# Seven products for eight of the sixteen k tiles instead of four, in nine tile pairs of a SwiGLU feed-forward

## The chip, the cores and the metric

The kernel runs on one core of a Trainium2 chip, as one launch. The metric is the device time of that core in microseconds. The core has a matrix engine (TensorE, PE in the rows), two engines that do elementwise work (VectorE, or DVE, and ScalarE, or ACT), a third one for it, GpSimd (POOL), and SyncE (SP), which here issues nearly all transfers. The engines run at the same time and wait for each other through semaphores.

## The reference

One layer of a decoder trunk for 256 tokens of width 2048, in float32: a sparse latent attention, and after it a SwiGLU feed-forward with 5632 hidden columns, each followed by a residual sum and a LayerNorm. The change touches only the feed-forward:

```python
def _swiglu(x, w_gate, w_up, w_down):
    return (jax.nn.silu(x @ w_gate) * (x @ w_up)) @ w_down
# of the layer:
x = _layer_norm(DEEPNORM_ALPHA * x + m, ln1_g, ln1_b)
x = _layer_norm(DEEPNORM_ALPHA * x + _swiglu(x, w_gate, w_up, w_down), ln2_g, ln2_b)
```

## The kernel before

**Three matmuls for each product.** TensorE takes its operands in the format F32R, so every float32 operand is kept as two parts: a high part, rounded by a ScalarE copy, and a low part, the rest, which VectorE gets by subtracting the high part from the float32 value. A product is high by high, high by low and low by high. The stationary operand is a 128 x 128 tile of the activations (act_t, s_t), the moving one 512 columns of the weights (w_hi, w_lo).

**Halves and the ring.** Weights arrive by DMA in raw. They are split in pieces of 1024 columns for each partition, called halves here: one ScalarE instruction writes w_hi, one VectorE instruction writes w_lo. Both have room for RING = 4 halves. Half v is split into the place of half v - 4, so ScalarE waits until TensorE has used that one; VectorE waits for ScalarE (hi_done), TensorE for VectorE (lo_done). SyncE's loads wait for lo_done as well, since raw is free when the low part is made.

**Tiles and pairs.** Gate and up are computed in 22 tiles of 256 hidden columns (512 columns of weights with gate and up side by side), over 16 k tiles of 128. Tiles 0 and 1 are computed on their own. The other 20 form ten pairs (p = 1 to 10). A pair has two tiles and two groups of 128 tokens, so it is a 2 x 2 block problem for every two k tiles. Of the 16 k tiles, the first four of each pair are done in the form of Strassen and Winograd: seven block products instead of eight. The sums of activations that this needs (s_t: s1 to s4) are made once, by GpSimd, ahead of pair 1. The sums of weight blocks (t_sum, four of them for each pair) are made by VectorE, in place in raw, between the low parts. Each of the seven product halves is used by 6 matmuls, and each of the 12 plain halves (the other 12 k tiles, for both tiles) by 12. Three ScalarE copies between PSUM banks (seed), one to p5_s, and two VectorE additions of p5_s bring the seven products to the four results.

**What else these engines do in a pair.** Twice for each pair: ScalarE applies silu (silu_step), VectorE multiplies gate by up (gate_up), TensorE transposes the result by four small matmuls (turn_hid), ScalarE and VectorE split the transposed tile into hid_t (hid_hi, hid_lo). All of it is written into the engines' instruction streams by hand, between the halves, and every engine works in order.

**Memory.** xn holds the normalized activations x1 for the residual sum at the end, s_t has its own place, and raw has five slots of 1 MB in this phase: three for plain weights, two for the blocks of the products. Earlier phases use the first four. So one of the two block slots of pair 1 is free only when tile 1 has been split.

## Time and profile before

| | |
|---|---|
| median of 3 runs | 963.92 us (963.87 to 964.64) |
| the profiled execution | 964.98 us, of which its span (first to last instruction) 962.8 us |
| TensorE | busy 949.2 us, 4536 matmuls |
| VectorE | busy 624.6 us |
| ScalarE | busy 486.4 us |
| GpSimd | busy 52.2 us |
| transfers | 183.84 MB, mean 191 GB/s |

An instruction's duration is longer than its share of the time where an engine works on two at once: a matmul of 512 columns is listed with 389 ns in the middle of a pair, but the next one starts sooner than that. So what a group of instructions costs is read from starts, or from the chain that ended last, where instructions in a row are merged. The engine tables give what an engine did; whether that matters depends on whom it keeps waiting.

### The profile page before, as it was taken

To read this page: it belongs to the slowest core of one execution; us is meant where nothing else is said; L and a number is where in the kernel's file an instruction comes from. 1 tells how busy PE (TensorE), PEld (TensorE's weight loads), DVE (VectorE), ACT (ScalarE), POOL (GpSimd) and SP (SyncE) were. 2 spreads that over 40 slices of the span, in tenths; PEclk is the share of its full clock that TensorE was granted. 3 is DMA by queue.
4 is the path that set the end of the run, shared out by engine and by line. 5 is a ranking of instruction groups with operands and counts; after the bars stand their busy time and mean duration, and the time that the engine had idled before them with its cause. 6 is when DMAs were issued, how large, how long until landed. Compare 5 with 4: busy or idle time off the path is not lost.

```text
span 962.8 us, 11466 instructions
## 1 busy us (share of the span) xinstructions
PE 949.2 (99%) x4536; PEld 794.4 (83%) x4536; DVE 624.6 (65%) x750; ACT 486.4 (51%) x644; POOL 52.2 (5%) x49
## 2 busy tenths in 40 slices
PE   9999999999969999999999999999999999999997
PEld 8999988888848888888888888888888888888885
DVE  6687666587556868586776858576745454444556
ACT  5677764452435646464655646364544343343450
POOL 0115520000400000000000000000000000000000
PEclk9999999999969999999999999999999999999999
DMA  9734315592326364654636364553457455464532
GB/s 364 315 136 175 122 55 214 180 392 88 132 87 262 124 270 166 228 197 152 235 115 268 136 253 185 208 216 133 164 206 288 172 220 180 170 225 168 219 131 88
DMA packets 28147, 183.84 MB, mean 191 GB/s; under 512 B 3136, under 2 KB 3648, under 8 KB 8640
## 3 DMA queue, kind: packets, MB, share of 16 engines
q1 hardware_dynamic: 28064, 183.12, 50.5%
q8 instruction: 36, 0.59, 0.2%
q14 instruction: 15, 0.12, 0.0%
q0 software_dynamic: 32, 0.00, 0.0%
HBM read 181.01 MB, written 2.10 MB: 190 GB/s over the span
## 4 chain that ended last, share of the span: by engine, by line
PE 70%; DVE 1%; DMA 0%; ACT 0%; issue 0%; DVEq 0%; ACTq 0%
PE acc L1782 26%; PE acc L1561 25%; PE tp L1782 8%; PE acc L1769 6%; PE tp L1769 4%; PE tp L1738 1%; DMA raw<-in_w_pairs 0%; DVE raw L1254 0%; PE acc L1867 0%; DVE w_lo L1090 0%; DVE w_lo L1242 0%; ACT w_hi L836 0%; ACT w_hi L755 0%; DVE stats L1326 0%; ACT acc L851 0%
## 5 line engine op out<-in xcount | busy, mean ns | idle before, releaser
L1090 DVE TENSOR_TENSOR w_lo<-raw,w_hi 128x1024 fp32r<-128x1024 f32 (+1 forms) x123 | 146.1, 1195 | 133.8 <-ACT w_hi L755 133.1
L1782 PE MATMUL acc<-w_hi,act_t 128*128 128x512 f32 x720 | 227.1, 392 | 0.0
L1561 PE MATMUL acc<-w_hi,hid_t 128*128 128x512 f32 x672 | 207.9, 389 | 0.0
L1249 DVE TENSOR_TENSOR w_lo<-raw,w_hi 128x1024 fp32r<-128x1024 f32 x120 | 145.2, 1224 | 95.8 <-ACT w_hi L845 94.7
L755 ACT ACTIVATE w_hi<-raw 128x1024 fp32r<-128x1024 f32 x116 | 115.9, 1001 | 164.7 <-PE acc L1561 152.3
L845 ACT ACTIVATE w_hi<-raw 128x1024 fp32r<-128x1024 f32 x120 | 126.1, 1060 | 126.3 <-PE acc L1782 111.2
L1782 PEld LDWEIGHTS acc<-w_hi,act_t 128*128 128x128 f32 x720 | 135.2, 188 | 27.8
L1561 PEld LDWEIGHTS acc<-w_hi,hid_t 128*128 128x128 f32 x672 | 126.1, 188 | 26.1
L1782 PE MATMUL acc<-w_lo,act_t 128*128 128x512 f32 x360 | 140.2, 389 | 0.0
L1561 PE MATMUL acc<-w_lo,hid_t 128*128 128x512 f32 x336 | 130.7, 389 | 0.0
L836 ACT ACTIVATE w_hi<-raw 128x1024 fp32r<-128x1024 f32 x70 | 72.9, 1057 | 74.4 <-DVE raw L1254 48.5
L1242 DVE TENSOR_TENSOR w_lo<-raw,w_hi 128x1024 fp32r<-128x1024 f32 x70 | 83.9, 1222 | 35.1 <-ACT w_hi L836 34.0
L1782 PEld LDWEIGHTS acc<-w_lo,act_t 128*128 128x128 f32 x360 | 67.7, 188 | 13.6
L1782 PE MATMUL tp<-w_hi,act_t 128*128 128x512 f32 x240 | 74.7, 389 | 0.0
L1561 PEld LDWEIGHTS acc<-w_lo,hid_t 128*128 128x128 f32 x336 | 63.1, 188 | 13.1
L1561 PE MATMUL acc<-w_hi,o_t 128*128 128x512 f32 x224 | 73.4, 398 | 0.0
L1782 PEld LDWEIGHTS tp<-w_hi,act_t 128*128 128x128 f32 x240 | 45.1, 188 | 9.3
L1561 PEld LDWEIGHTS acc<-w_hi,o_t 128*128 128x128 f32 x224 | 42.1, 188 | 8.6
L1254 DVE TENSOR_TENSOR raw<-raw 128x1024 f32<-128x1024 f32 x40 | 47.9, 1219 | 0.0
L1782 PE MATMUL tp<-w_lo,act_t 128*128 128x512 f32 x120 | 46.7, 389 | 0.0
L1561 PE MATMUL acc<-w_lo,o_t 128*128 128x512 f32 x112 | 43.6, 390 | 0.0
L1769 PE MATMUL acc<-w_hi,act_t 128*128 128x512 f32 x100 | 36.9, 410 | 6.6 <-DVE w_lo L1242 6.6
(226 smaller groups left out, 1273.3 us busy)
## 6 DMA issues: line engine op xcount, KB each, us to landing
raw<-in_w_pairs SPq DMA_DIRECT2D x80, 1024.0 KB, 4.7
raw<-in_w_down SPq DMA_DIRECT2D x32, 1024.0 KB, 4.6
raw<-in_w_out SPq DMA_DIRECT2D x16, 1024.0 KB, 4.8
raw<-in_w_down SPq DMA_DIRECT2D x16, 768.0 KB, 4.0
raw<-in_w_gu SPq DMA_DIRECT2D x8, 1024.0 KB, 7.0
raw<-in_x_w SPq DMA_DIRECT2D x14, 552.0 KB, 6.9
raw<-in_w_uq SPq DMA_DIRECT2D x4, 1024.0 KB, 6.3
raw<-in_w_ukv SPq DMA_DIRECT2D x4, 1024.0 KB, 5.7
```

The costliest lines, as they stand in the source:

```text
L755: act.activation(w_hi[:, (2 * slot + half + shift) % RING, 0:n], raw[:, slot, first:first + n], ACT.Copy).then_inc(hi_done, 1)
L836: act.activation(by_quad(w_hi[:, v_pair(p, n) % RING, :]), quad(block), ACT.Copy).then_inc(hi_done, 1)
L845: act.activation(w_hi[:, v_pair(p, n) % RING, :], raw[:, slot, h % 2 * HALF:(h % 2 + 1) * HALF], ACT.Copy).then_inc(hi_done, 1)
L1090: dve.tensor_tensor(w_lo[:, h, 0:n], raw[:, slot, first:first + n], w_hi[:, h, 0:n], ALU.subtract).then_inc(lo_done, 1)
L1242: dve.tensor_tensor(by_quad(w_lo[:, v % RING, :]), quad(block), by_quad(w_hi[:, v % RING, :]), ALU.subtract).then_inc(lo_done, 1)
L1249: dve.tensor_tensor(w_lo[:, v % RING, :], raw[:, h // 2 % PAIR_RING, h % 2 * HALF:(h % 2 + 1) * HALF], w_hi[:, v % RING, :], ALU.subtract) ...
L1254: dve.tensor_tensor(quad(dst), quad(x), quad(y), ALU.add).then_inc(t_done, 1)
L1561: last = pe.matmul(acc[:, bank0 + t, :], lhs[:, k, x, t * P:(t + 1) * P], part[:, w, n * GC:(n + 1) * GC], start=(start and x == 0 and par ...
L1738: last = pe.transpose(turned[:, c, t * P:(t + 1) * P], hid[:, t, c * P:(c + 1) * P], ident[:])
L1769: last = pe.matmul(out, factor(q, what, x), part[:, v % RING, q * GC:(q + 1) * GC], start=(start and (q, x) == (0, 0) and part is w_hi), s ...
L1782: last = pe.matmul(out[:, t, :], act_t[:, k0 + m, x, t * P:(t + 1) * P], part[:, v % RING, m * GC:(m + 1) * GC], start=False, stop=((h % P ...
```

## The change

In pairs 2 to 10 the seven products cover eight k tiles instead of four (GROUPS_OF is 1 for pair 1 and 2 for the others). A pair then has 14 product halves (product n for block group 0, then for group 1) and 8 plain halves. The block weights get four slots of raw that are theirs alone, the plain weights four places of 512 KB. For the room this takes, s_t lies where xn is; x1 is written to the output tensor in DRAM after it is made, and read back into xn after the products of pair 10. GpSimd makes the activation sums in two rounds, the second during the plain halves of pair 1. Silu, gate_up, and the transposes with their splits stand at other halves. The diff, cut:

```diff
-QUADS = 2
-PAIR_K = 2 * QUADS
+QUADS = 4
 B11, B21, B12, B22 = range(4)
+T1, T3, T2, T4 = range(4)
 S1, S2, S3, S4 = range(4)
+GROUPS_OF = (None, 1) + (2,) * (PAIRS - 2)
 PRODUCTS = 7
-PLAIN = (KD - PAIR_K) // 2
-PAIR_HALVES = PRODUCTS + 2 * PLAIN
-PAIR_RING = 3
-PLAIN_LOADS = PLAIN
-PAIR_SIGNALS = PAIR_HALVES - 2
+PLAIN_SLOTS = 4
+
+
+def products(p):
+    return PRODUCTS * GROUPS_OF[p]
+
+
+def plain_halves(p):
+    return KD - 4 * GROUPS_OF[p]
+
+
+def halves(p):
+    return products(p) + plain_halves(p)
+
+
 V_FFN = 2 * R_FFN
 V_PAIRS = V_FFN + 2 * TILE_HALVES
-V_DOWN = V_PAIRS + PAIR_HALVES * (PAIRS - 1)
+V_PAIR = (None,) + tuple(V_PAIRS + sum(halves(q) for q in range(1, p)) for p in range(1, PAIRS + 1))
...
         xn = sb("xn", [P, TOK, D])
+        s_t = nc.alloc_sbuf_tensor_at("s_t", [P, 2, 4, QUADS, P], F32R, offset=base_x)
...
-            def load_quads(p):
-
-                if p > 1:
-                    sp.wait_ge(lo_done, v_pair(p - 1, PRODUCTS))
-                for q in range(QUADS):
-                    if p == 1 and q == 0:
...
+            def load_quad(p, n):
+                q = quad_slots(p)[n]
+                if p == 1:
+                    pass
+                elif p == 2 and q < 2:
+                    sp.wait_ge(lo_done, V_FFN + TILE_HALVES + 2 * (PLAIN_SLOTS // 2 + q) + 2)
+                else:
+                    sp.wait_ge(lo_done, v_pair(p - 1, products(p - 1)))
+                sp.dma_start(raw[:, PLAIN_SLOTS // 2 + q, :], w_pairs[p - 1][:, n * RAW_ELEMS:(n + 1) * RAW_ELEMS])\
+                  .then_inc(quad_full[q], 16)
...
+                m = PLAIN_BEFORE[p] + n
+                if m < PLAIN_SLOTS:
+                    sp.wait_ge(lo_done, V_FFN + TILE_HALVES + m + 1)
                 else:
-                    sp.wait_ge(lo_done, V_FFN + TILE_HALVES + 2 * n + 2)
-                e0 = (QUADS + n) * RAW_ELEMS
-                sp.dma_start(raw[:, n % PAIR_RING, :], w_pairs[p - 1][:, e0:e0 + RAW_ELEMS])\
-                  .then_inc(raw_full[n % PAIR_RING], 16)
-
-            for p in range(1, PAIRS):
-                if p == 1:
-                    load_plain(p, 0)
-                    load_plain(p, 1)
-                    load_plain(p, 2)
-                    load_quads(p)
-                else:
-                    for n in range(PAIR_RING):
-                        load_plain(p, n)
-                if p < PAIRS - 1:
-                    load_quads(p + 1)
-                for n in range(PAIR_RING, PLAIN_LOADS):
-                    load_plain(p, n)
+                    sp.wait_ge(lo_done, plain_v(m - PLAIN_SLOTS) + 1)
+                e0 = 2 * GROUPS_OF[p] * RAW_ELEMS + n * HALF
+                sp.dma_start(plain_raw(m), w_pairs[p - 1][:, e0:e0 + HALF]).then_inc(plain_full[m % PLAIN_SLOTS], 16)
...
+            load_quad(1, 0)
+            load_quad(1, 1)
+            for n in range(PLAIN_SLOTS):
+                load_plain(1, n)
+            sp.wait_ge(x1_done, TOK * CHUNKS)
+            sp.dma_start(a["out"].rearrange("(t p) d -> p t d", p=P), xn[:]).then_inc(x1_stored, 16)
+            for p in range(1, PAIRS):
+                if p > 1:
+                    for n in range(PLAIN_SLOTS):
+                        load_plain(p, n)
+                for n in range(PLAIN_SLOTS, plain_halves(p)):
+                    load_plain(p, n)
+                    if p < PAIRS - 1:
+                        if n - PLAIN_SLOTS < 2 * GROUPS_OF[p + 1]:
+                            load_quad(p + 1, n - PLAIN_SLOTS)
+                    elif n - PLAIN_SLOTS < 2:
+                        load_down(0, n - PLAIN_SLOTS)
+
+            for b in range(2, RING):
                 load_down(0, b)
+            sp.wait_ge(x1_stored, 16)
+            sp.wait_ge(*used_half(v_pair(PAIRS - 1, products(PAIRS - 1))))
+            sp.dma_start(xn[:], a["out"].rearrange("(t p) d -> p t d", p=P)).then_inc(x1_back, 16)
...
+                seeds = {G + 3: (0, first[:, 0, :], 1.0), 3 * G + 3: (2, second[:, 0, :], -1.0),
+                         5 * G + 3: (4, first[:, 1, :], 1.0)}
+                for j in range(halves(p)):
...
                         if p > 1:
                             hid_hi(2 * p - 2)
                         silu_step(2 * p - 1)
-                    if h == 9:
+                    if j == 5 * G + 4:
                         hid_hi(2 * p - 1)
+                    if j == n_products + plain_halves(p) // 2 + 3:
                         silu_step(2 * p)
+                    if p == 1 and j == n_products + 6:
...
+            def hid_chores(p, j):
+
+                if j == 5:
+                    if p > 1:
+                        hid_lo(2 * p - 2)
+                    gate_up(2 * p - 1)
+                if j == 5 * GROUPS_OF[p] + 4:
+                    hid_lo(2 * p - 1)
+                if j == products(p) + plain_halves(p) // 2 + 3:
+                    gate_up(2 * p)
...
-                lo_product(p, 0, B11)
-                t_sum(B11, B11, B12)
-                t_sum(B12, B12, B22)
-                lo_product(p, 1, B11)
-                t_sum(B11, B11, B22)
-                lo_product(p, 2, B11)
-                lo_product(p, 3, B21)
-                t_sum(B21, B11, B21)
-                lo_product(p, 4, B12)
-                lo_product(p, 5, B22)
-                lo_product(p, 6, B21)
...
+                groups = range(GROUPS_OF[p])
+                for n in range(PRODUCTS):
+                    for g in groups:
+                        lo_product(p, n, g)
+                        if n == 0:
+                            t_sum(p, g, B11, B11, B12)
+                        if n == 3:
+                            t_sum(p, g, B21, B11, B21)
+                        hid_chores(p, GROUPS_OF[p] * n + g)
+                    for g in groups:
+                        if n == 0:
+                            t_sum(p, g, B12, B12, B22)
+                        if n == 1:
+                            t_sum(p, g, B11, B11, B22)
...
+            for g in range(2):
+                if g == 1:
+                    pool.wait_ge(lo_done, v_pair(1, products(1)))
+                k = act_t[:, 4 * g:4 * g + 4, :, :].rearrange("p (q k) x s -> p q k x s", q=2)
+                x1, s_g = x1_t[:, g, :, :, :], s_sum[:, g, :, :, :]
...
+                for g in range(GROUPS_OF[p]):
+                    v = v_pair(p, GROUPS_OF[p] * n + g)
+                    if v == v_pair(p, 1) and p > 1:
+                        turn_hid(2 * p - 2)
+                    pe.wait_ge(lo_done, v + 1)
+                    for n_q in range(2):
+                        for x, part in ((0, w_hi), (0, w_lo), (1, w_hi)):
+                            end = (g, n_q, x) == (GROUPS_OF[p] - 1, 1, 1)
+                            last = pe.matmul(out, factor(2 * g + n_q, what, x),
+                                             part[:, v % RING, n_q * GC:(n_q + 1) * GC],
+                                             start=(start and (g, n_q, x) == (0, 0, 0) and part is w_hi),
+                                             stop=end, skip_group_check=not start)
+                    last.then_inc(pe_used, 1)
 
...
-                for h in range(PLAIN):
-                    if h == 0 and p > 1:
-                        turn_hid(2 * p - 2)
-                    if h == 5:
+                n = plain_halves(p) // 2
+                for h in range(n):
+                    if h == 0:
                         turn_hid(2 * p - 1)
                     plain(p, h, first)
                 pe.wait_ge(p5_added, 2 * p)
-                for h in range(PLAIN, 2 * PLAIN):
+                for h in range(n, 2 * n):
                     plain(p, h, second)
 
```

VectorE, one pair from the middle of the ten, before. L1242 is the low part of a product half, L1254 a sum of weight blocks, L1249 the low part of a plain half, L1228 hid_lo, L1224 gate_up, L1279 and L1281 the additions of p5_s.

```order
L1242 TENSOR_TENSOR w_lo<-raw,w_hi 128x1024
L1254 TENSOR_TENSOR raw<-raw 128x2x512 x2
L1242 TENSOR_TENSOR w_lo<-raw,w_hi 128x1024
L1254 TENSOR_TENSOR raw<-raw 128x2x512
L1242 TENSOR_TENSOR w_lo<-raw,w_hi 128x1024 x2
L1254 TENSOR_TENSOR raw<-raw 128x2x512
L1242 TENSOR_TENSOR w_lo<-raw,w_hi 128x1024 x3
L1249 TENSOR_TENSOR w_lo<-raw,w_hi 128x1024 x4
L1228 TENSOR_TENSOR hid_t<-tp,hid_t 128x2x256
L1224 TENSOR_TENSOR hid<-hid,tp 128x512
L1249 TENSOR_TENSOR w_lo<-raw,w_hi 128x1024
L1279 TENSOR_TENSOR acc<-p5_s,acc 128x512
L1281 TENSOR_TENSOR acc<-p5_s,acc 128x512
L1249 TENSOR_TENSOR w_lo<-raw,w_hi 128x1024 x5
L1228 TENSOR_TENSOR hid_t<-tp,hid_t 128x2x256
L1249 TENSOR_TENSOR w_lo<-raw,w_hi 128x1024
L1224 TENSOR_TENSOR hid<-hid,acc 128x512
```

The same place now. L1298 is the low part of a product half, L1309 a sum, L1305 the low part of a plain half, L1282 hid_lo, L1278 gate_up.

```order
L1298 TENSOR_TENSOR w_lo<-raw,w_hi 128x1024
L1309 TENSOR_TENSOR raw<-raw 128x2x512
L1298 TENSOR_TENSOR w_lo<-raw,w_hi 128x1024
L1309 TENSOR_TENSOR raw<-raw 128x2x512 x3
L1298 TENSOR_TENSOR w_lo<-raw,w_hi 128x1024 x2
L1309 TENSOR_TENSOR raw<-raw 128x2x512 x2
L1298 TENSOR_TENSOR w_lo<-raw,w_hi 128x1024 x2
L1282 TENSOR_TENSOR hid_t<-tp,hid_t 128x2x256
L1278 TENSOR_TENSOR hid<-hid,tp 128x512
L1298 TENSOR_TENSOR w_lo<-raw,w_hi 128x1024
L1309 TENSOR_TENSOR raw<-raw 128x2x512
L1298 TENSOR_TENSOR w_lo<-raw,w_hi 128x1024
L1309 TENSOR_TENSOR raw<-raw 128x2x512
L1298 TENSOR_TENSOR w_lo<-raw,w_hi 128x1024 x6
L1305 TENSOR_TENSOR w_lo<-raw,w_hi 128x1024
L1282 TENSOR_TENSOR hid_t<-tp,hid_t 128x2x256
```

Ahead of the last low part of a product half there were 4 sums and no other work; now there are 8 sums, a hid_lo and a gate_up, and 14 low parts instead of 7. The second hid_lo follows the first plain half at once.

SyncE's queue where the pairs begin, before. L479 loads tiles 0 and 1, L534 plain weights, L521 block weights.

```order
L479 DMA raw<-in_w_gu 128x2048 [waits lo_done] x8
L534 DMA raw<-in_w_pairs 128x2048 [waits lo_done] x3
L521 DMA raw<-in_w_pairs 128x2048 [waits lo_done]
L521 DMA raw<-in_w_pairs 128x2048
L521 DMA raw<-in_w_pairs 128x2048 [waits lo_done]
L521 DMA raw<-in_w_pairs 128x2048
L534 DMA raw<-in_w_pairs 128x2048 [waits lo_done] x6
```

The same place now. L514 loads tiles 0 and 1, L558 block weights, L569 plain weights, L588 stores x1.

```order
L514 DMA raw<-in_w_gu 128x2048 [waits lo_done] x8
L558 DMA raw<-in_w_pairs 128x2048 x2
L569 DMA raw<-in_w_pairs 128x1024 [waits lo_done] x4
L588 DMA out<-xn 128x2x2048 [waits x1_done]
L569 DMA raw<-in_w_pairs 128x1024 [waits lo_done]
L558 DMA raw<-in_w_pairs 128x2048 [waits lo_done]
L569 DMA raw<-in_w_pairs 128x1024 [waits lo_done]
L558 DMA raw<-in_w_pairs 128x2048 [waits lo_done]
```

The two block loads of pair 1 now stand ahead of its plain loads and wait for nothing but the queue; the store of x1 is new; the four block loads of pair 2 alternate with plain loads.

## Rows read from the trace of the kernel before

**Rows 1.** The page: span, and busy time of each engine.

```profile
span 962.8 us, 11466 instructions
...
PE 949.2 (99%) x4536; PEld 794.4 (83%) x4536; DVE 624.6 (65%) x750; ACT 486.4 (51%) x644; POOL 52.2 (5%) x49
```

**Rows 2.** Stages: start:end, length, busy (count) of PE PEld DVE ACT POOL, PEclk, DMA.

```profile
269.80:326.40 56.60, 48.78 (x192) 38.84 (x192) 36.21 (x33) 26.20 (x29) 0.00 (x0) 0.85 0.46 174
...
369.60:412.80 43.20, 43.20 (x196) 35.76 (x195) 30.89 (x30) 23.65 (x29) 0.00 (x0) 1.00 0.51 195
```

**Rows 3.** Chain that ended last, the first pair: start us, us, what.

```profile
266.91 4.68 DMA raw<-in_w_pairs
...
275.18 1.23 DVE w_lo L1242
...
283.60 9.79 PE acc L1769 x30
...
293.39 13.60 PE acc L1782 x60
```

**Rows 4.** The same chain, two later pairs.

```profile
499.01 4.08 PE tp L1769 x18
...
508.53 0.44 PE tp L1738 x4
...
508.97 13.65 PE acc L1782 x60
...
544.85 6.80 PE acc L1769 x30
...
585.26 4.08 PE tp L1769 x18
```

**Rows 5.** TensorE in windows of 4 us: length, busy (count), PEclk, DMA share, GB/s.

```profile
268.00:272.00 4.00, 1.98 (x9) 1.00 0.97 385
...
272.00:276.00 4.00, 0.00 (x0) 0.53 0.29 121
...
284.00:288.00 4.00, 4.00 (x10) 0.50 0.00 0
```

**Rows 6.** VectorE in order of time: start us, us, line, operation, count, idle.

```profile
492.06 1.22 DVE L1242 TENSOR_TENSOR w_lo<-raw,w_hi 128x1024 fp32r<-128x1024 f32 x1 [1.57 <-ACT w_hi L836]
...
493.20 2.36 DVE L1254 TENSOR_TENSOR raw<-raw 128x1024 f32<-128x1024 f32 x2
...
510.84 0.68 DVE L1228 TENSOR_TENSOR hid_t<-tp,hid_t 128x512 fp32r<-128x512 f32 x1
...
511.44 0.68 DVE L1224 TENSOR_TENSOR hid<-hid,acc 128x512 f32<-128x512 f32 x1
```

**Rows 7.** ScalarE in order of time, the same pair.

```profile
490.97 1.06 ACT L836 ACTIVATE w_hi<-raw 128x1024 fp32r<-128x1024 f32 x1 [1.74 <-PE acc L1782]
...
500.96 2.00 ACT L836 ACTIVATE w_hi<-raw 128x1024 fp32r<-128x1024 f32 x2
...
502.86 0.59 ACT L871 ACTIVATE p_s<-tp 128x512 f32<-128x512 f32 x1
```

**Rows 8.** TensorE in order of time: start of product half 0; after the wait.

```profile
498.85 0.39 PE L1769 MATMUL tp<-w_hi,act_t 128*128 128x512 f32 x1
...
276.56 0.76 PE L1769 MATMUL acc<-w_hi,act_t 128*128 128x512 f32 x1 [6.58 <-DVE w_lo L1242]
```

**Rows 9.** TensorE, ScalarE, GpSimd and VectorE in tile 1.

```profile
261.15 0.60 PE L1738 MATMUL tp<-ident,hid 128*128 128x128 f32 x4
...
261.79 0.60 ACT L820 ACTIVATE hid_t<-tp 128x512 fp32r<-128x512 f32 x1 [4.76 <-PE tp L1738]
...
263.41 2.40 POOL L1398 TENSOR_TENSOR s_t<-s_sum,s_t 128x1024 fp32r<-128x1024 f32 x1 [10.61 <-ACT s_t L831]
...
264.31 2.58 DVE L1090 TENSOR_TENSOR w_lo<-raw,w_hi 128x1024 fp32r<-128x1024 f32 x1 [1.20 <-ACT w_hi L755]
```

**Rows 10.** Issues of transfers: count, KB each, median us to landing.

```profile
xn<-in_x SPq DMA_DIRECT2D x1, 2048.0 KB, 14.3
```

More of the change, by code:

```diff
@@ L554, in load_down @@
-                if isinstance(g, int) and n < RING:
-                    n_pair = PRODUCTS if slot == PAIR_RING else PRODUCTS + 2 * (slot + PAIR_RING) + 2
-                    sp.wait_ge(lo_done, v_pair(PAIRS - 1, n_pair))
+                slot, n = down_slot(b), DOWN_BLOCKS * g + b
+                if isinstance(g, int) and n < 2:
+                    sp.wait_ge(lo_done, v_pair(PAIRS - 1, products(PAIRS - 1)))
+                elif isinstance(g, int) and n < RING:
+                    sp.wait_ge(lo_done, V_DOWN - PLAIN_SLOTS + 2 * slot + 2)
@@ L747, in _, with hi_loop @@
                     hi_static(SPLIT_OF[s])
-            def hi_loop(used, raw_count, half, slot, n=HALF, first=None, shift=0):
+            def hi_loop(used, raw_count, half, slot, n=HALF, first=None):
                 first = half * n if first is None else first
@@ L754, in hi_loop @@
                 act.wait_ge(*used)
-                act.activation(w_hi[:, (2 * slot + half + shift) % RING, 0:n], raw[:, slot, first:first + n],
+                act.activation(w_hi[:, (2 * slot + half) % RING, 0:n], raw[:, slot, first:first + n],
                                ACT.Copy).then_inc(hi_done, 1)
@@ L1270, in lo_pair @@
-                for h in range(2 * PLAIN):
-                    lo_plain(p, h)
-                    if h == 3:
-                        if p > 1:
-                            hid_lo(2 * p - 2)
-                        gate_up(2 * p - 1)
-                    if h == 4:
+                groups = range(GROUPS_OF[p])
[8 more added lines that the diff above has]
+                    for g in groups:
+                        if n == 0:
+                            t_sum(p, g, B12, B12, B22)
+                        if n == 1:
+                            t_sum(p, g, B11, B11, B22)
@@ L1277, in lo_pair @@
+                for h in range(plain_halves(p)):
+                    lo_plain(p, h)
+                    hid_chores(p, products(p) + h)
+                    if h == 2:
                         dve.wait_ge(p5_done, p)
-                        dve.wait_ge(*used_pair(p, 5))
+                        dve.wait_ge(*used_half(v_pair(p, 6 * GROUPS_OF[p] - 1)))
                         dve.tensor_tensor(second[:, 0, :], p5_s[:], second[:, 0, :], ALU.add).then_inc(p5_added, 1)
@@ L1763, in strassen @@
             def strassen(p, n, what, out, start):
-                v = v_pair(p, n)
-                pe.wait_ge(lo_done, v + 1)
-                for q in range(QUADS):
-                    for x, part in ((0, w_hi), (0, w_lo), (1, w_hi)):
-                        last = pe.matmul(out, factor(q, what, x), part[:, v % RING, q * GC:(q + 1) * GC],
-                                         start=(start and (q, x) == (0, 0) and part is w_hi),
-                                         stop=((q, x) == (QUADS - 1, 1)), skip_group_check=not start)
-                last.then_inc(pe_used, 1)
+                for g in range(GROUPS_OF[p]):
+                    v = v_pair(p, GROUPS_OF[p] * n + g)
+                    if v == v_pair(p, 1) and p > 1:
[9 more added lines that the diff above has]
+                    last.then_inc(pe_used, 1)
             def plain(p, h, out):
-                n = PRODUCTS + h
-                v, k0 = v_pair(p, n), PAIR_K + 2 * (h % PLAIN)
+                tile, n = divmod(h, plain_halves(p) // 2)
+                v, k0 = v_pair(p, products(p) + h), 4 * GROUPS_OF[p] + 2 * n
+                end = n == plain_halves(p) // 2 - 1
                 pe.wait_ge(lo_done, v + 1)
@@ L1892 @@
     later = gu[2:].reshape(PAIRS - 1, 2, P, KD, 2 * FC)
-    quads = later[:, :, :, 0:PAIR_K].reshape(PAIRS - 1, 2, P, QUADS, 2, 2 * FC).transpose(0, 2, 3, 1, 4, 5)
-    plain = later[:, :, :, PAIR_K:].transpose(0, 2, 1, 3, 4).reshape(PAIRS - 1, P, -1)
+    w_pairs = []
+    for p in range(1, PAIRS):
+        n_k = 4 * GROUPS_OF[p]
+        quads = later[p - 1][:, :, 0:n_k].reshape(2, P, n_k // 2, 2, 2 * FC).transpose(1, 2, 0, 3, 4)
+        plain = later[p - 1][:, :, n_k:].transpose(1, 0, 2, 3)
+        w_pairs.append(np.concatenate([quads.reshape(P, -1), plain.reshape(P, -1)], axis=1))
     arrays = {
```

236 lines of the change are left out of this document (121 added, 115 removed).

## Prediction, made before the run

> **What bounds the kernel now.** I read the page first: TensorE is busy 949.2 of 962.8 us [rows 1], so nearly everything counts by what it does to TensorE. Its busy time is no price, though, since matmuls overlap. The chain that ended last shows the pace: 60 matmuls of plain halves in 13.65 us and 30 of product halves in 6.80 us [rows 4], 0.227 us each. A plain half (12 matmuls) thus costs 2.73 us, a product half (6) 1.36, four transposes 0.44. Two pairs of before, from 499.01 to 585.26, take 86.25 us [rows 4], 43.1 each; 186 matmuls and eight transposes make 42.3 + 0.9 = 43.2. A pair in the middle has no hole.
>
> The stage table shows the one exception: pair 1 takes 56.6 us with a granted clock of 0.85, a later one 43.2 at 1.00 [rows 2]. The chain tells why: a load of block weights is issued at 266.91, the low part of product half 0 starts at 275.18 [rows 3], and TensorE's first matmul starts at 276.56 after 6.58 us of idle time [rows 8]. The clock is 0.53 in the window of that hole and still 0.50 from 284 to 288, with TensorE busy throughout [rows 5]: the lower of its two levels (1.2 GHz, not 2.4). So 30 matmuls took 9.79 us instead of 6.80 [rows 3]. Tile 1 ended at 269.8 (start of the stage of [rows 2]), the seven products at 293.39 [rows 3]: 23.6 us for 42 matmuls that are worth 9.5. The hole and the slow clock cost 14.1 us.
>
> **Term 1, fewer matmuls.** In pairs 2 to 10 a second group of four k tiles goes from 48 matmuls to 42: 186 become 180. 9 x 6 x 0.227 = 12.3 us less.
>
> **Term 2, the second load of pair 1.** It now has a slot of its own and stands ahead of the plain loads, so it is there when tile 1 ends. But VectorE is late at that point. ScalarE does hid_hi at 261.79, then the split of s_t, then half 7; GpSimd's subtraction at 263.41 runs beside VectorE's half 7, which starts at 264.31 and takes 2.58 us instead of 1.22 [rows 9, 6]. From 266.8 on VectorE has half 0, two sums, half 1, a sum, half 2: with its pace below, half 2 is ready at 275.0, where TensorE, starting at 269.8, would want it at 272.5. I walk the rest likewise (half 3 at 276.1, half 4 at 278.4, half 6 at 281.3) and get products that end at 282.8 instead of 279.3: 3.5 us of waits remain. GpSimd's second round then falls beside the low parts of the next plain halves; at twice their duration, as in the row above, they take about as long as TensorE's 2.73, and I add 1 us. Gain 14.1 - 4.5, so 9.6 us. Bounds: 14 if nothing of that shows, 5 if the new store of x1 is late: it is issued after tile 1's half 3 (about 252), and if it takes the 14.3 us of the other 2 MB transfer [rows 10] it lands at 266.5, 4.3 us after ScalarE asks for it (262.3).
>
> **Term 3, VectorE in the product halves.** Before, the seven halves (9.5 us of TensorE) had 11 VectorE instructions of 1024 columns. Now 14 halves (19.1 us) have 22, and a hid_lo and a gate_up. Paces: starts of such instructions in a row are 1.14 us apart (492.06 to 493.20), of the small ones 0.60 (510.84 to 511.44) [rows 6]; ScalarE's are 0.95 (500.96 to 502.86 for two) [rows 7]. Hand-overs: ScalarE's copy of half 0 starts at 490.97 [rows 7], 0.31 after TensorE leaves the plain half four back (498.85 [rows 8] less three plain halves, 490.66), its end 492.03 releases VectorE at 492.06 [rows 6], and VectorE's end at 276.41 releases TensorE at 276.56 [rows 3, 8]: 0.31, 0.03 and 0.15. A big VectorE instruction takes 1.22 to its end, ScalarE's 1.06.
>
> Time 0 is where TensorE starts a pair's half 0. The ring lets VectorE begin it only at -6.8. From there: half 0 and a sum, half 1 from -4.1 (its place is free one plain half later, so 0.45 is lost), three sums, half 2 from 0.5, half 3 from 1.6, two sums until 5.1; half 4 ends at 6.3, half 5 at 7.8 (0.3 lost, as ScalarE copies a PSUM bank before it), then hid_lo and gate_up, half 6 ends at 10.1, half 7 at 12.4, half 8 at 14.7. TensorE, at 1.36 a half and a transpose in between, would want half 4 at 5.9. It starts it at 6.5, half 6 at 10.3, half 7 at 12.5, half 8 at 14.8; after that VectorE has one instruction for each half (1.14 against 1.36) and waits end. The product halves end at 23.0 instead of 19.5: **3.5 us of waits**, nearly all in four pieces of 0.6 to 1.0.
>
> Then ScalarE, after half 14, waits for the transposes that now stand right before it on TensorE. In tile 1 such a copy started 0.64 us after the transposes did [rows 9]. Then half 15 is split: 0.64 + 0.48 + 1.06 + 0.03 + 1.22 + 0.15 = 3.6 us, against 0.44 + 2.73 = 3.2 on TensorE: **0.4 us**. Restarts after idle time are a little slower; with 0.1 for them a pair loses 4.0 us. The plain halves then let VectorE get four ahead again (the last eight take 21.8 us of TensorE, 11.5 us of VectorE), so every pair starts alike. 9 x 4.0 = 36 us.
>
> Bounds. Below: without the losses at halves 1 and 5 the walk gives 2.7 + 0.3 = 3.0, so 27 us. Above: if the hand-overs cost VectorE its whole 1.22 for each of the 16 big instructions ahead of half 8, another 1.3: 48 us. Nothing is excluded as a gain here, since no row shows two block groups. I take 4.0, as the starts in [rows 6] are of just these two kinds.
> One rule speaks to this. The Trainium skill ("VectorE: DVE Perf Modes", section on the DRAIN) says that the next instruction does not start until the pipe of the one before is empty; by that the starts would be 1.22 apart, and the sum would be 12 us higher. The rows disagree by 0.08 us for each instruction, and I follow them.
>
> **At nothing:** the same bytes are loaded, 8 MB a pair, now in 45 to 47 us. But four block loads of a pair are issued between low parts 14 and 17 (21.8 to 29.9 of the walk); at the 385 GB/s that a busy window shows [rows 5] the 4.5 MB behind low part 15 are through at about 40, where ScalarE asks at 40.7. No cover is left there; late by 1 us, it costs 1 us a pair, which the upper bound holds. Silu and gate_up are done 9 us or more ahead of the transposes that need them. The read of x1 goes out four plain halves before the down projection and is wanted a column group later.
>
> **Sum.** Against the profiled execution (964.98 us, span 962.8): -12.3 - 9.6 + 36 = +14.1. On the median of 963.92 that is 978.
>
> **Rivals.**
> - The waits stay small (other side). Place: VectorE's order from product half 0 to 8. If it finished half 8 as early as TensorE wants it (11.3 instead of 14.7), nothing would be lost, as before, where 11 instructions in 9.5 us caused no wait. All hidden gives 963.9 - 12.3 - 9.6 = 942. It decides at 2.4 us a pair (21.9 / 9). For: this phase is covered before. Against: it would need VectorE to start before the ring lets it, or 0.9 us for each instruction. 0.12 for faster at all, 0.05 for within 0.2% (waits of 2.2 to 2.6).
> - The clock falls in each pair. Place: halves 4 to 8, where TensorE would be idle more than a third of the time. Each product half after it at the lower level costs 1.2 us more (30 matmuls in 9.79 us are already a mixture; half the clock doubles 1.36). Six of them less what the waits hide, about 5 to 7 us a pair: 1025 to 1040. For: after the one long hole the clock stayed low for more than 10 us [rows 5, 3]. Against: no row shows a hole under 1 us that lowers it. 0.08. The Trainium skill ("TensorE: Matmul & The Clock Gate", second failure mode) describes such short pauses between groups of matmuls that make the clock swing; nothing in this trace shows it.
> - Pair 1 keeps its hole, because the block loads or the x1 store are late: term 2 is then near nothing, 988. 0.06, inside the range.
>
> My forecast has 0.69. Slower is that, the clock and pair 1 together, 0.83. Range: 966 (lower bound of term 3, whole gain in pair 1: 963.9 - 12.3 - 14 + 27 = 964.6) to 994 (963.9 - 12.3 - 5 + 48); below I go to 962 to take in part of the close cases. Left out are most of the faster case and the clock case, less than 0.2. 0.2% is about 2 us, what a measurement of this kernel can tell from no change.
>
> **What would show it.** In the trace of after: TensorE's hole before pair 1 gone and the clock at 1.00 throughout; 54 matmuls fewer; in each of pairs 2 to 10 waits of TensorE for w_lo, the first at half 4 and the last at half 8, about 3.5 us together, and one of 0.4 after the first plain half; pairs of 45.8 us instead of 43.1; VectorE without idle time through the product halves. The prediction is wrong if VectorE's starts are closer than 1.14, if it gets more than four halves ahead, if ScalarE (seeds, silu, hid_hi) and not VectorE is late, or if a load is.

## The result, and the profile after

The changed kernel takes **991.96 us** (median of 4 runs, 991.34 to 993.49) against 963.89 (963.78 to 964.64): 2.9% slower, ratio 1.0293 with a 95% interval of 1.0277 to 1.0309. Direction and range of the prediction held. The size did not: the change costs 28.1 us, and the forecast was 14.1, half of that.

The page of the changed kernel, with its transfers (to be held against [rows 1] and [rows 10]):

```profile
span 989.6 us, 11576 instructions
...
PE 946.0 (96%) x4482; PEld 775.6 (78%) x4482; DVE 692.6 (70%) x813; ACT 508.8 (51%) x672; POOL 65.0 (7%) x55
...
L900 ACT ACTIVATE w_hi<-raw 128x1024 fp32r<-128x1024 f32 x84 | 85.7, 1054 | 81.2 <-DMA raw<-in_w_pairs 78.4
...
raw<-in_w_pairs SPq DMA_DIRECT2D x84, 512.0 KB, 6.6
raw<-in_w_pairs SPq DMA_DIRECT2D x38, 1024.0 KB, 8.3
```

The 54 matmuls are gone, and TensorE's share of the span is 96% instead of 99%. The line that the prediction did not expect is L900, ScalarE's copy of plain weights: it waits 78.4 us for transfers.

The stages of the changed kernel, cut within 0.3 us of the starts of product half 0 (columns as in [rows 2]):

```profile
270.30:316.80 46.50, 43.91 (x193) 35.23 (x192) 34.59 (x32) 25.44 (x29) 12.83 (x6) 1.00 0.60 226
...
411.00:741.30 330.30, 303.14 (x1316) 237.99 (x1315) 266.07 (x251) 181.58 (x210) 0.00 (x0) 1.00 0.45 175
741.30:989.60 248.30, 243.20 (x1071) 199.82 (x1069) 128.65 (x133) 95.52 (x101) 0.29 (x1) 1.00 0.52 191
```

Pair 1 ends at 316.80 and not at 326.40, a gain of 9.6 us, and its clock is 1.00 instead of 0.85. The last seven pairs take 330.30 us, and all nine from 316.80 to 741.30 take 424.5: **47.17 each in the mean**, where before it was 43.1 (the stretch to 714.6 in the run before is 388.2 us). That is 36.3 us more. What follows the pairs takes the same time as before (248.3 us against 248.2). So the spans of the two profiled executions differ by 36.3 - 9.6 + 0.1 = 26.8 us, and the whole surplus is in pairs 2 to 10. (The medians differ by 28.1: the profiled execution of before is 1.1 us above its median, that of the changed kernel 0.6 below.)

The nine pairs are not alike. Pair 2 takes what the prediction said for every pair; the next eight take 47.3 each. The first two rows are stages (columns as in [rows 2]); the last two, from the chain, are the starts of product half 8 in pairs 2 and 3, 47.97 us apart:

```profile
316.75:362.49 45.74, 43.22 (x189) 34.11 (x188) 36.13 (x35) 26.02 (x30) 0.00 (x0) 1.00 0.47 184
362.49:741.20 378.71, 347.08 (x1506) 272.36 (x1504) 306.08 (x288) 207.87 (x240) 0.00 (x0) 1.00 0.45 175
...
331.56 5.70 PE tp L1842 x24
...
379.53 8.44 PE acc L1842 x36
```

TensorE in one of these eight pairs, pair 7, from the start of its product half 0 (columns as in [rows 8]):

```profile
551.88 0.39 PE L1842 MATMUL acc<-w_hi,act_t 128*128 128x512 f32 x1
...
559.83 0.47 PE L1842 MATMUL acc<-w_hi,s_t 128*128 128x512 f32 x1 [1.64 <-DVE w_lo L1298]
...
563.52 0.50 PE L1842 MATMUL acc<-w_hi,act_t 128*128 128x512 f32 x1 [0.69 <-DVE w_lo L1298]
...
565.79 0.50 PE L1842 MATMUL acc<-w_hi,act_t 128*128 128x512 f32 x1 [0.62 <-DVE w_lo L1298]
...
568.16 0.47 PE L1842 MATMUL acc<-w_hi,s_t 128*128 128x512 f32 x1 [0.71 <-DVE w_lo L1298]
```

The waits stand at halves 4, 6, 7 and 8, where the walk put them (three of the eight pairs have one of 0.4 to 0.7 us at half 2 too). But half 4 starts 7.95 us after half 0, not 6.5, and half 8 16.28 instead of 14.8. From half 4 to half 8 it is 8.33 us, as forecast (8.3); half 4 itself comes 1.4 us late, and that delay stays. VectorE, just before, shows why:

```profile
547.03 1.22 DVE L1298 TENSOR_TENSOR w_lo<-raw,w_hi 128x1024 fp32r<-128x1024 f32 x1
548.16 1.22 DVE L1309 TENSOR_TENSOR raw<-raw 128x1024 f32<-128x1024 f32 x1
```

It begins product half 0 at 547.03, 4.85 us ahead of TensorE; the walk had 6.8. The chain that ended last leads to the reason:

```profile
529.81 2.77 PE acc L1857 x12
532.58 1.21 DVE w_lo L1305
...
536.14 8.03 DMA raw<-in_w_pairs
544.20 1.07 ACT w_hi L900
545.29 1.23 DVE w_lo L1305
...
547.12 1.14 DVE w_lo L1298
```

The last plain load of the pair, 512 KB, is issued at 536.14 and lands after 8.03 us. ScalarE and VectorE wait for it at the end of the plain halves, just when VectorE should get ahead. In the windows around it the 16 DMA engines are busy all the time (length, clock, DMA share, GB/s):

```profile
536.00:540.00 4.00, 1.00 1.01 406
540.00:544.00 4.00, 1.00 1.02 424
```

The Trainium skill ("DMA: Bandwidth & Descriptors", section on queues, rings and completion order) says that each DMA engine takes the descriptors of one ring in order. The trace agrees as far as it goes: SyncE has issued three of its four 1 MB block loads (the first two at 528.31 and 533.05) ahead of that load, and it lands late behind them. It can't tell waiting in a ring from sharing full engines. The row of the third block load and its own (start, time to issue, line):

```profile
534.29 0.60 SPq L558 DMA_DIRECT2D raw<-in_w_pairs  x1
536.14 0.33 SPq L569 DMA_DIRECT2D raw<-in_w_pairs  x1
```

That pair 2 starts in time fits: pair 1 has twelve plain halves, of 2.7 us of TensorE each, to load the four blocks of pair 2 in, and pairs 2 to 9 have eight.

### The profile page after: what moved, and what is told of

Read it like the earlier page. It is cut to its first block, busy times and chain, and to the rows that moved or that the text cites. A ratio compares the mean times of both kernels' runs of the same rounds, so it can differ in the third digit from the quotient of the medians.

```text
span 989.6 us, 11576 instructions
## 1 busy us (share of the span) xinstructions
PE 946.0 (96%) x4482; PEld 775.6 (78%) x4482; DVE 692.6 (70%) x813; ACT 508.8 (51%) x672; POOL 65.0 (7%) x55
## 4 chain that ended last, share of the span: by engine, by line
PE 67%; DVE 22%; DMA 7%; ACT 3%; issue 2%; ACTq 0%; DVEq 0%; SPq 0%
PE acc L1630 33%; DVE w_lo L1298 8%; PE acc L1857 8%; DVE raw L1309 7%; DMA raw<-in_w_pairs 6%; PE acc L1842 5%; PE acc L1568 5%; PE acc L1489 4%; PE tp L1842 3%; DVE w_lo L1305 3%; PE acc L1767 2%; ACT w_hi L892 1%; PE acc L1602 1%; DVE w_lo L1144 1%; DMA out<-xn 1%
## 5 line engine op out<-in xcount | busy, mean ns | idle before, releaser
L1162 DVE TENSOR_TENSOR w_lo<-raw,w_hi 128x1024 fp32r<-128x1024 f32 x92 | 103.8, 1132 | 115.9 <-ACT w_hi L952 115.1
L1857 PE MATMUL acc<-w_hi,act_t 128*128 128x512 f32 x512 | 162.9, 393 | 1.3
L1298 DVE TENSOR_TENSOR w_lo<-raw,w_hi 128x1024 fp32r<-128x1024 f32 x133 | 158.4, 1221 | 5.7 <-ACT w_hi L892 5.7
L1305 DVE TENSOR_TENSOR w_lo<-raw,w_hi 128x1024 fp32r<-128x1024 f32 x84 | 101.9, 1235 | 60.9 <-ACT w_hi L900 60.5
L900 ACT ACTIVATE w_hi<-raw 128x1024 fp32r<-128x1024 f32 x84 | 85.7, 1054 | 81.2 <-DMA raw<-in_w_pairs 78.4
L1857 PEld LDWEIGHTS acc<-w_hi,act_t 128*128 128x128 f32 x512 | 96.1, 188 | 24.6 <-DVE w_lo L1305 5.1
L1857 PE MATMUL acc<-w_lo,act_t 128*128 128x512 f32 x256 | 99.8, 390 | 0.0
L1309 DVE TENSOR_TENSOR raw<-raw 128x1024 f32<-128x1024 f32 x76 | 90.3, 1219 | 0.0
L1842 PE MATMUL acc<-w_hi,act_t 128*128 128x512 f32 x188 | 66.8, 404 | 11.6 <-DVE w_lo L1298 11.6
L1842 PE MATMUL tp<-w_hi,s_t 128*128 128x512 f32 x196 | 65.4, 398 | 12.2 <-DVE w_lo L1298 12.2
L1842 PEld LDWEIGHTS tp<-w_hi,s_t 128*128 128x128 f32 x196 | 36.7, 187 | 26.9 <-issue 10.9
L1842 PEld LDWEIGHTS acc<-w_hi,act_t 128*128 128x128 f32 x188 | 35.3, 188 | 26.5 <-DVE w_lo L1298 19.4
L1857 PEld LDWEIGHTS acc<-w_lo,act_t 128*128 128x128 f32 x256 | 48.1, 188 | 9.5
L1144 DVE TENSOR_TENSOR w_lo<-raw,w_hi 128x1024 fp32r<-128x1024 f32 x31 | 42.4, 1383 | 18.5 <-ACT w_hi L797 18.5
L1857 PE MATMUL tp<-w_hi,act_t 128*128 128x512 f32 x160 | 50.1, 389 | 0.0
```

Of the source, the lines that this page charges most:

```text
L900: act.activation(w_hi[:, v % RING, :], plain_raw(m), ACT.Copy).then_inc(hi_done, 1)
L1144: dve.tensor_tensor(w_lo[:, h, :], raw[:, slot, half * HALF:(half + 1) * HALF], w_hi[:, h, :], ALU.subtract).then_inc(lo_done, 1)
L1162: dve.tensor_tensor(dst, raw[:, slot, half * HALF:half * HALF + n], src_hi, ALU.subtract).then_inc(lo_done, 1)
L1298: dve.tensor_tensor(by_quad(w_lo[:, v % RING, :]), quad(p, g, LOW_OF[n]), by_quad(w_hi[:, v % RING, :]), ALU.subtract).then_inc(lo_done, 1)
L1305: dve.tensor_tensor(w_lo[:, v % RING, :], plain_raw(PLAIN_BEFORE[p] + h), w_hi[:, v % RING, :], ALU.subtract).then_inc(lo_done, 1)
L1309: dve.tensor_tensor(quad(p, g, dst), quad(p, g, x), quad(p, g, y), ALU.add).then_inc(t_done, 1)
```

## The experiments

In all of them before was run on the same chip: 964.48 us (963.61 to 965.3, 7 runs) for the first four kernels, 963.84 (963.42 to 965.17, 7 runs) for the others. Each kernel has 4 runs. Diffs are cut, and are against the changed kernel except for the last.

**No block loads for pairs 3 to 10.** The products of these pairs use old contents of raw.

```diff
-            return sum(q in quad_slots(n) for n in range(1, p + 1))
+            return sum(q in quad_slots(n) for n in range(1, min(p, 2) + 1))
...
                     sp.wait_ge(lo_done, v_pair(p - 1, products(p - 1)))
+                if p > 2:
+                    return
```

> Leaves out: the block weights of pairs 3 to 10 are not loaded, the products of these pairs work on what pair 2 left in the four block slots. Every instruction of the four compute engines stays. Theory A (plain loads queue behind the block loads, land late, and cost VectorE part of its lead; 1.4 us in each of pairs 2 to 10 on top of the 4.0 of the walk): plain loads land in 5 us or less, no ScalarE wait for w_pairs in pairs 3 to 9, pairs of 45.8 us instead of 47.2, time about 992 - 12 = 980. Theory B (the missing 1.4 us is VectorE's or ScalarE's own pace, or the restart of TensorE, loads don't matter): 990 to 992.

Measured: 979.55 us, ratio 1.0156 (1.0139 to 1.0173). The plain loads land after 4.5 us instead of 6.6 (medians). ScalarE still waits 36.7 us for plain weights, where theory A had none in pairs 3 to 9, but those waits come earlier in the pair and VectorE makes them good. The same rows of TensorE and VectorE in this kernel:

```profile
546.46 0.39 PE L1844 MATMUL acc<-w_hi,act_t 128*128 128x512 f32 x1
...
552.94 0.47 PE L1844 MATMUL acc<-w_hi,s_t 128*128 128x512 f32 x1 [0.38 <-DVE w_lo L1300]
...
556.63 0.51 PE L1844 MATMUL acc<-w_hi,act_t 128*128 128x512 f32 x1 [0.70 <-DVE w_lo L1300]
```
```profile
539.68 1.23 DVE L1300 TENSOR_TENSOR w_lo<-raw,w_hi 128x1024 fp32r<-128x1024 f32 x1 [0.92 <-ACT w_hi L894]
...
542.40 1.23 DVE L1300 TENSOR_TENSOR w_lo<-raw,w_hi 128x1024 fp32r<-128x1024 f32 x1 [0.36 <-ACT w_hi L894]
```

The chain's rows of this kernel give half 8 of two pairs in a row and the transposes after the product halves:

```profile
515.53 5.71 PE tp L1844 x24
...
523.96 0.45 PE tp L1809 x4
...
561.26 8.41 PE acc L1844 x36
```

This is the walk of the prediction, nearly to the tenth:

| us from TensorE's half 0 | predicted | no block loads | the change |
|---|---|---|---|
| VectorE begins half 0 | -6.8 | -6.78 | -4.85 |
| VectorE begins half 1 | -4.1 | -4.06 | -2.58 |
| TensorE half 4 | 6.5 | 6.48 | 7.95 |
| TensorE half 6 | 10.3 | 10.17 | 11.64 |
| TensorE half 7 | 12.5 | 12.44 | 13.91 |
| TensorE half 8 | 14.8 | 14.80 | 16.28 |
| a whole pair | 45.8 | 45.73 | 47.20 |

The last column is pair 7; pair 2 of the changed kernel agrees with the middle column to 0.02 us on TensorE (half 4 at 6.48, half 8 at 14.81, 45.74 in all). Late loads are worth 991.96 - 979.55 = 12.4 us (13.2 by the two ratios). The edit changes eight pairs, 3 to 10, so that is 1.6 for each; from the traces it is 47.34 - 45.73. Pair 1 is no part of it: in the trace of this run it is 1.2 us longer than in the changed kernel, at a lower clock (last section).

**No sums of weight blocks.** All calls of t_sum are left out, and the waits for them; the products are then made with the blocks as they are.

```diff
-            SUM_OF = {1: T1, 2: T2, 4: T3, 6: T4}
+            SUM_OF = {}
...
-                        if n == 0:
-                            t_sum(p, g, B11, B11, B12)
...
```

> Leaves out: the sums of weight blocks (76 VectorE instructions), so the products use blocks that are not summed. Theory A (VectorE's work in the product halves makes the waits there): TensorE has no waits at the product halves, only about 0.4 us at the second plain half of each of pairs 2 to 10, although the loads are still late; pairs of 42.2 us, time about 963.9 - 12.3 - 9.6 + 3.6 = 946. Theory B (late loads alone would stop TensorE): waits stay, over 955.

Measured: 945.30 us, ratio 0.9793 (0.9777 to 0.9810). The loads are as late as in the change:

```profile
L900 ACT ACTIVATE w_hi<-raw 128x1024 fp32r<-128x1024 f32 x84 | 85.7, 1055 | 85.0 <-DMA raw<-in_w_pairs 83.5
```

With 76 VectorE instructions less, no matmul in the pairs waits for L1298 any more, and pairs 2 to 10 take 42.33 us each, as theory A has it. So late loads cost time here only because VectorE has no time to make good what it loses.

**The second hid_hi and hid_lo two halves later.**

```diff
-                    if j == 5 * G + 4:
+                    if j == n_products + 2:
                         hid_hi(2 * p - 1)
...
-                if j == 5 * GROUPS_OF[p] + 4:
+                if j == products(p) + 2:
                     hid_lo(2 * p - 1)
```

> Same result as the changed kernel; the second hid_hi and hid_lo of a pair stand after the third plain half instead of the first. Theory A (ScalarE's wait for the transposes costs 0.4 us directly, and holds low part 15 and with it the loads that wait for it back by 3.5 us, which is what makes the plain loads late): the wait at the second plain half is gone, the loads start 3.5 us earlier, pairs of 45.4 us, time about 976 (-1.8 us a pair). Theory B (the lateness is the transfers' rate and stays): only the 0.4 us go, 988.

Measured: 985.03 us, ratio 1.0212 (1.0195 to 1.0229), 6.9 us less than the change. That lies between the two expectations, nearer to B. Pair 2, which no late load holds up, shows the wait by itself. It takes 45.31 us here and 45.74 in the changed kernel:

```profile
317.12:362.43 45.31, 42.95 (x189) 34.20 (x188) 36.53 (x35) 26.37 (x30) 0.00 (x0) 1.00 0.47 186
```

That is the 0.4 us that the prediction named, some 3.9 in nine pairs. The other 3 us lie in pairs 3 to 10 (46.49 each instead of 47.34). An earlier start of the loads would explain them, since low part 15 no longer waits for the transposes. But ScalarE still waits 79.1 us for plain weights here, so this edit alone does not bring them in time.

**One group in all pairs.** The slots, the loads in turn, the second round of sums and the store of x1 stay as in the change; the number of products is that of before.

```diff
-GROUPS_OF = (None, 1) + (2,) * (PAIRS - 2)
+GROUPS_OF = (None,) + (1,) * (PAIRS - 1)
```

> Same result; all ten pairs have one block group as before the change, everything else (slots, queue, x1 through DRAM, places of silu and transposes) as changed. Theory A (the second group alone costs 9 x (5.4 - 1.4) us, the rest of the change gains 9.6 in pair 1): pairs 2 to 10 of 43.2 us without waits, time about 954. Theory B (the smaller plain loads or the moved silu and transposes cost something by themselves): 958 or more, with waits of TensorE in pairs 2 to 10.

Measured: 957.71 us, ratio 0.9931 (0.9914 to 0.9947), so **faster than before**. The time lies between the two expectations. Two of its pairs, from 403.53 to 490.46, take 86.93 us, 43.47 each, against 43.1. The 0.3 us stand in the product halves, where 12 matmuls take 2.77 and 2.91 instead of 2.72 (chain of this kernel):

```profile
405.33 2.77 PE tp L1842 x12
...
409.46 2.91 PE tp L1842 x12
```

A hid_lo and a gate_up, with hid_hi and silu on ScalarE, now lie between these halves; no run tested whether they are the cause. Here too ScalarE waits 69.1 us for plain weights, and it costs TensorE nothing, since VectorE has time in hand.

**The plain loads ahead of the block loads.** Block load 0 stays behind plain load 4, the other three go behind plain load 7.

```diff
-                    if p < PAIRS - 1:
-                        if n - PLAIN_SLOTS < 2 * GROUPS_OF[p + 1]:
-                            load_quad(p + 1, n - PLAIN_SLOTS)
+                    behind = {PLAIN_SLOTS: (0,), PLAIN_SLOTS + 3: (1, 2, 3)}.get(n, ())
+                    for q in behind:
+                        if p < PAIRS - 1:
+                            load_quad(p + 1, q)
...
```

> Same result; only SyncE's order in a pair changes: three of the four block loads of the next pair stand behind the last plain load instead of between the plain loads. Theory A (late plain loads cost VectorE's lead): no more than short waits of ScalarE for w_pairs in the last plain halves, pairs of 45.8 us, time about 980, as in the run that loads no blocks. Theory B (the transfers are too many for the time in any order, so the block loads are late instead): 986 or more, and ScalarE waits for w_pairs at product half 0 or 1.

Measured: 1000.63 us, ratio 1.0373 (1.0355 to 1.0390), slower than the change, as theory B has it. The last plain half is split 10.6 us before the next pair again (at 546.02, pair at 556.64), but the block weights come late. ScalarE and VectorE before the second half of a pair:

```profile
553.72 2.01 ACT L893 ACTIVATE w_hi<-raw 128x1024 fp32r<-128x1024 f32 x2 [3.90 <-DMA raw<-in_w_pairs]
```
```profile
554.82 1.23 DVE L1299 TENSOR_TENSOR w_lo<-raw,w_hi 128x1024 fp32r<-128x1024 f32 x1 [2.60 <-ACT w_hi L893]
```

So this order does not help by itself (no third one was run): all of these loads have to pass between the moment that raw comes free and the start of the next pair. The next experiment lets them start earlier.

**Both: that order, and hid_hi and hid_lo later.** Of the two diffs together, the lines that set the places:

```diff
+                    behind = {PLAIN_SLOTS: (0,), PLAIN_SLOTS + 3: (1, 2, 3)}.get(n, ())
...
-                    if j == 5 * G + 4:
+                    if j == n_products + 2:
...
-                if j == 5 * GROUPS_OF[p] + 4:
+                if j == products(p) + 2:
```

> Same result; this order of loads, and hid_hi and hid_lo after the third plain half. Theory A: the wait at the second plain half goes too, and the loads start 3.5 us earlier: pairs of 45.4 us, time about 976. Theory B: 982 or more.

Measured: 977.39 us, ratio 1.0132 (1.0113 to 1.0150). The one edit alone costs 8.7 us, the other alone brings 6.9, and together they bring 14.6. Theory A's 976 is nearly met. The edits help each other: with low part 15 made before the transposes are used, loads can begin earlier, and the order that cost time now brings some; that the earlier start is the reason is argued and not measured. This is the best version with two groups and the right result that was run, and it is still 13.6 us slower than before.

**A part of the sums on GpSimd.** The kernel of the experiment above, with the sum of blocks 12 and 22 moved from VectorE to GpSimd, 19 in all.

```diff
...
+            def pool_sums(p):
+                for g in range(GROUPS_OF[p]):
+                    pool.wait_ge(t_done, T_BEFORE[p] + g + 1)
+                    pool.tensor_tensor(quad(p, g, B12), quad(p, g, B12), quad(p, g, B22),
+                                       ALU.add).then_inc(pool_sum, 1)
...
```

> Same result; as e6_both, and the two sums of blocks 12 and 22 of each pair are made by GpSimd instead of VectorE. GpSimd took 2.4 us for 1024 columns, and VectorE 2.6 instead of 1.2 for the instruction beside it. Theory A (VectorE is slowed as much as it is relieved): VectorE's low parts beside the two sums take 2 us and more, time 972 to 982, no gain. Theory B (relief counts in full, 2 x 1.14 us a pair): 976 - 20 = 956.

Measured: 993.93 us, ratio 1.0307 (1.0290 to 1.0324), 16.5 us slower than without it: no gain, as theory A says, but a loss far beyond its 972 to 982. VectorE and GpSimd at the start of one pair:

```profile
548.37 1.23 DVE L1302 TENSOR_TENSOR w_lo<-raw,w_hi 128x1024 fp32r<-128x1024 f32 x1 [0.92 <-ACT w_hi L896]
...
551.48 2.81 DVE L1302 TENSOR_TENSOR w_lo<-raw,w_hi 128x1024 fp32r<-128x1024 f32 x1 [0.75 <-ACT w_hi L896]
...
555.35 4.54 DVE L1302 TENSOR_TENSOR w_lo<-raw,w_hi 128x1024 fp32r<-128x1024 f32 x2
...
556.56 3.33 DVE w_lo L1302
```
```profile
550.81 2.40 POOL L1456 TENSOR_TENSOR raw<-raw 128x1024 f32<-128x1024 f32 x1 [39.18 <-DVE raw L1313]
555.51 3.30 POOL L1456 TENSOR_TENSOR raw<-raw 128x1024 f32<-128x1024 f32 x1 [2.30 <-DVE raw L1313]
```

Two sums left VectorE, 2.3 us at its pace. Beside GpSimd, a low part takes 2.81 us instead of 1.23, and two in a row 4.54 instead of 2.36: 3.8 us are lost, more than was taken off. (The last VectorE row is from the chain: the second of the two.) The rows show whole instructions in turn. GpSimd's first addition ends at 553.21, and the low part that VectorE had started at 551.48 ends at 554.29, 1.08 us later, as if only then begun. The second addition starts at 555.51 beside a low part that ends at 556.56 as usual; it ends at 558.81, 2.25 us after that, and the next low part at 559.89, again 1.08 later. In all 19 of these additions the low part that was started beside one ends 1.08 to 1.09 us after it, however long it is listed with (2.43 to 3.36 us). The Trainium skill ("SBUF — State Buffer", section on who interferes with whom) says that a VectorE instruction with two inputs in SBUF contends with a GpSimd instruction that reads SBUF, for a port that is locked exclusively. The trace agrees, by these ends.

**The kernel before, with block slots of its own.** One group, and none of the other edits: raw has RING + 2 slots of 1 MB, the two block loads of pair 1 stand ahead of its plain loads and wait for nothing. The room is that of s_t, which lies in a part of hid_t that is written later. The diff is against before:

```diff
-        raw = sb("raw", [P, PAIR_RING + QUADS, RAW_ELEMS])
+        raw = sb("raw", [P, RING + QUADS, RAW_ELEMS])
...
-                    if p == 1 and q == 0:
-                        sp.wait_ge(lo_done, V_FFN + 2 * TILE_HALVES)
-                    sp.dma_start(raw[:, PAIR_RING + q, :],
+                    sp.dma_start(raw[:, RING + q, :],
...
+                    load_quads(p)
                     load_plain(p, 0)
                     load_plain(p, 1)
                     load_plain(p, 2)
-                    load_quads(p)
```

> Same result; the kernel before with one thing of the change: six slots of raw, so that the two block loads of pair 1 have slots of their own and stand ahead of the plain loads. s_t takes the room of the last two tiles of hid_t, so x1 makes no trip through DRAM, and silu, transposes and one block group are as before. If pair 1 loses only what VectorE is late by (about 3 us): 963.9 - 14.1 + 3 = 953. Rival: the 3.8 us by which the run with one group everywhere is slower than my 954 are in pair 1 too and not in the moved silu and transposes: 957.

Measured: 954.03 us, the median of three runs between 953.79 and 955.10; a fourth took 5464.2 us, which nothing here explains (the median of all four is 954.57). The ratio is 0.9893 (0.9873 to 0.9913), and this is the fastest kernel of all that give the right result. Pair 1, and a later one, in the profiled execution:

```profile
269.80:316.64 46.84, 44.56 (x191) 36.18 (x190) 32.83 (x31) 24.24 (x28) 0.00 (x0) 0.96 0.49 180
359.76:402.89 43.13, 43.13 (x196) 35.70 (x195) 30.87 (x29) 23.61 (x27) 0.00 (x0) 1.00 0.53 196
```

Pair 1 ends at 316.64 instead of 326.40, and later pairs are what they were. It has the gain of term 2 without the price of term 3. The rival is answered too: the run with one group everywhere leaves pair 1 at the same time (316.43, here 316.47), so 3.1 of the 3.7 us that it is slower by lie in its later pairs, 0.34 us in each of nine.

## Why the prediction was right, and where it was wrong

**Term 1, right.** 4482 matmuls instead of 4536. A pair of the first experiment, 45.73 us, is 180 x 0.227 + 0.9 plus 4.0 of waits.

**Term 2, right in size, by two misses that cancel.** Pair 1 ended 9.6 us earlier, as forecast, and 9.8 in the last experiment. The hole of 6.58 us is gone and the clock is 1.00 in the window that had 0.53. What remains are waits of 0.34, 1.94 and 0.31 us, and the products end at 283.78, where I had 282.8:

```profile
267.55 1.21 DVE L1298 TENSOR_TENSOR w_lo<-raw,w_hi 128x1024 fp32r<-128x1024 f32 x1
...
279.30 4.48 PE acc L1842 x18
283.78 0.44 PE tp L1807 x4
284.21 27.28 PE acc L1857 x120
```

VectorE begins half 0 at 267.55, where the walk had 266.8, and the delay stays. The low bound's cause was half true, and it is where that delay comes from. The store of x1 took 10.9 us, not 14.3, and ScalarE waited 1.15 us for it:

```profile
263.00 1.06 ACT L878 ACTIVATE s_t<-s_sum 128x1024 fp32r<-128x1024 f32 x1 [1.15 <-DMA out<-xn]
```

TensorE then waited 0.98 us in tile 1, and pair 1 began at 270.54 instead of 269.8: 0.7 us, where the bound had over 4 for it. The 1 us for GpSimd's second round does not show: the plain halves after 284.21 run on without a gap, 120 matmuls in 27.28 us. So the products end 1.0 us later than forecast, and 1 us that was forecast behind them is not there. That the sum came out to the tenth is luck.

**Term 3, VectorE's part right, late loads put at nothing: the step that failed.** The forecast was 36 us, 4.0 for each pair. The change has 47.17 - 41.74 = 5.4 in the mean, 48.8 for nine pairs. VectorE's walk is not at fault: without the block loads it holds at every row of the table, with 4.0 in all, and in the change itself it holds in pair 2. What failed is the sentence "The plain halves then let VectorE get four ahead again", and under it the paragraph **At nothing**. There I asked when the *last block load* is through (about 40) and when it is asked for (40.7), and called that just in time. I did not ask it of the plain loads that stand between and behind the block loads, and put them at nothing without a reason. That a load is late stood in the prediction as a sign of its being wrong, and it is what happened. In the first experiment ScalarE splits the last plain half 10.6 us before the next pair, at 35.1 of the walk:

```profile
535.84 1.06 ACT L902 ACTIVATE w_hi<-raw 128x1024 fp32r<-128x1024 f32 x1 [1.66 <-PE acc L1859]
```

In the change it does so 7.7 us before (544.20), so 2.9 us late. A slack of about 1 us in front of product half 0 takes up a part, VectorE starts it 1.9 us late, and 1.5 remain at half 4. In eight pairs the mean is 1.6, 12.8 us together, where the prediction had 0. The block loads were not quite in time either: ahead of three of the pairs (those that start at 410.48, 504.95 and 599.08) ScalarE waits 1.1 to 1.5 us for the block weights of half 1.

The sentence "late by 1 us, it costs 1 us a pair, which the upper bound holds" does not hold as it stands: 2.9 us late cost 1.5. Nor did the bound hold for term 3, 48.8 us against 48, and it had been made up from hand-overs, not from loads. That the total of 991.96 is inside the range, 2 us from its end, is due to the 4.6 us that the range kept for pair 1 and that were not needed: luck. (The lower end that the prediction calls 966 adds up to 964.6; nothing hangs on it.)

**The 0.4 us of the transposes, right.** With hid_hi and hid_lo moved, pair 2 is 0.43 us shorter (45.31 against 45.74).

**The pace of VectorE, right.** Low parts and sums start 1.13 to 1.14 us apart after the change too (547.03, 548.16). By the rule of the Trainium skill that was weighed ("VectorE: DVE Perf Modes", section on the DRAIN) they would be 1.22 apart. The trace disagrees. The same section adds that an instruction that is not held starts earlier, without a figure for it; here it is 0.08 us. By chance that larger sum (12 us more) would have come close to the result; the first experiment shows it would have been for a wrong reason.

**The rivals.** "The waits stay small" did not come about; without the sums it does (945.3 against its 942), so its deciding point was rightly VectorE's work between halves 0 and 8. "The clock falls in each pair" did not either: the granted clock is 1.00 in all stretches of the changed kernel, though TensorE is idle for 3.7 of the 10.0 us from 558.2 to 568.2. "Pair 1 keeps its hole" did not.

## What to carry to other kernels

When an edit puts large transfers in a queue, don't ask only whether they arrive in time: ask it of each small one that is issued between and behind them, at the moment that its reader wants it. An engine with time in hand hides a late transfer (one group: 69 us of waits for plain weights on ScalarE, and plain halves at TensorE's full pace), while one that has just been loaded to the brim hands on much of what it loses (2.9 us late, 1.5 lost), so a new bound and a late transfer have to be costed together. And an edit that bundles a gain with a price should be taken apart: the slots alone gain 9.8 us, the seven products for four more k tiles cost 34.
